# Recurrent core of a two-block network on one core: blocks of one shape put side by side on TensorE, value parts put behind both transposes

## What is computed

```python
def step(S, inp):
    r_t, w_t, k_t, v_t, kk_t, b_t = inp
    sa = jnp.einsum('bhvk,bhk->bhv', S, -kk_t)
    S = S * w_t[:, :, None, :] + sa[..., None] * b_t[:, :, None, :] + v_t[..., None] * k_t[:, :, None, :]
    return S, jnp.einsum('bhvk,bhk->bhv', S, r_t)
...
_, y = lax.scan(step, S0, tuple(to_time(t) for t in (rh, decay, kh, vh, kk, kk * ah)))
```

## Time and profile before

| | us |
|---|---|
| median of 3 runs | 1159.96 |
| lowest, highest | 1159.76, 1161.36 |
| profiled execution, its own time | 1160.52 |
| its span in the profile | 1158.3 |
| groups 0 to 3 of the core in the span | about 91 to 202 |
| PE busy | 1130.8 (98%) |

### The profile page before, as it was taken

One profiled execution on the slowest core, in us unless ns is written; L12 is line 12 of the kernel. 1 busy time (PEld: TensorE's weight loads), 2 busy tenths in 40 slices (PEclk: granted clock), 3 DMA queues, 4 the chain that ended last, 5 costly groups with the idle time before them and its releaser, 6 DMA issues.

```text
span 1158.3 us, 22050 instructions
## 1 busy us (share of the span) xinstructions
PE 1130.8 (98%) x9164; PEld 997.3 (86%) x9164; DVE 818.1 (71%) x1159; ACT 624.8 (54%) x923; POOL 132.3 (11%) x97
## 2 busy tenths in 40 slices
PE   7999999999999999999999999999999999999997
PEld 7797878778888889987888889999998998888886
DVE  7889886377666577898766666888587555666665
ACT  8984664464334455666543344575656655545443
POOL 0032364402300000220031000012000000000000
PEclk9999999999999999999999999999999999999999
DMA  8621211245544654334455447535434333554541
GB/s 306 227 98 51 64 56 57 70 168 183 217 171 165 246 218 146 146 112 180 166 198 218 182 159 267 191 110 218 167 126 151 141 146 145 200 194 171 217 177 41
DMA packets 29796, 187.17 MB, mean 162 GB/s; under 512 B 3472, under 2 KB 5648, under 8 KB 8592
## 3 DMA queue, kind: packets, MB, share of 16 engines
q1 hardware_dynamic: 27072, 177.21, 41.1%
q10 hardware_dynamic: 2640, 8.75, 2.4%
HBM read 184.90 MB, written 1.05 MB: 161 GB/s over the span
## 4 chain that ended last, share of the span: by engine, by line
PE 82%; DVE 10%; ACT 5%; issue 2%; DMA 1%; POOL 0%; DVEq 0%; SPq 0%; ACTq 0%; POOLq 0%
PE ps L2219 16%; PE ps L2201 16%; PE ps L2202 15%; PE ps L2203 15%; PE ps L2220 9%; DVE w_lo L1441 2%; PE ps L2718 1%; PE ps L2571 1%; DVE conv_out L2050 1%; ACT mixed L668 1%; PE ps L2560 1%; PE ps L2499 1%; PE ps L2965 1%; PE ps L2973 1%; PE ps L2451 1%
## 5 line engine op out<-in xcount | busy, mean ns | idle before, releaser
L1441 DVE TENSOR_TENSOR w_lo<-w_raw,w_hi 128x2048 fp32r<-128x2048 f32 x147 | 340.9, 2338 | 84.7 <-ACT w_hi L639 84.6
L639 ACT CAST w_hi<-w_raw 128x2048 fp32r<-128x2048 f32 x144 | 274.2, 1906 | 98.8 <-PE ps L2203 65.0
L2219 PE MATMUL ps<-x_both,w_hi 128*128 128x512 f32 x864 | 302.0, 392 | 1.4 <-DVE x_both L1739 0.6
L2220 PE MATMUL ps<-x_both,w_lo 128*128 128x256 f32 x864 | 243.9, 282 | 0.0
L2219 PEld LDWEIGHTS ps<-x_both,w_hi 128*128 128x128 f32 x864 | 162.2, 188 | 36.5 <-issue 1.5
L2220 PEld LDWEIGHTS ps<-x_both,w_lo 128*128 128x128 f32 x864 | 163.7, 189 | 1.1
L2201 PE MATMUL ps<-x_both,w_hi 128*128 128x256 f32 x432 | 122.0, 282 | 1.6 <-DVE w_lo L1441 0.9
L2202 PE MATMUL ps<-x_both,w_hi 128*128 128x256 f32 x432 | 120.8, 280 | 0.0
L2203 PE MATMUL ps<-x_both,w_lo 128*128 128x256 f32 x432 | 120.8, 280 | 0.0
L2201 PE MATMUL ps<-w_hi,hid_hi 128*128 128x512 f32 x304 | 118.8, 391 | 0.8 <-DVE hid_lo L1867 0.7
L2202 PE MATMUL ps<-w_lo,hid_hi 128*128 128x512 f32 x304 | 118.7, 390 | 0.0
(11 more groups left out here) (443 smaller groups left out, 2109.9 us busy)
## 6 DMA issues: line engine op xcount, KB each, us to landing
w_raw<-in_weights SPq DMA_DIRECT2D x163, 1024.0 KB, 5.0
xt<-in_xT SPq DMA_DIRECT2D x2, 512.0 KB, 5.8
w_raw<-in_weights SPq DMA_DIRECT2D x2, 512.0 KB, 6.6
x_tm<-in_x SPq DMA_DIRECT2D x1, 1024.0 KB, 5.0
gain<-in_mix_g ACTq DMA_DIRECT2D x2, 512.0 KB, 3.6
gain<-in_mix_b ACTq DMA_DIRECT2D x2, 512.0 KB, 5.3
gain<-in_ffn_g ACTq DMA_DIRECT2D x2, 512.0 KB, 5.6
gain<-in_ffn_b ACTq DMA_DIRECT2D x2, 512.0 KB, 9.3
```

Source lines behind the costliest of these rows:

```text
L639: nc.scalar.copy(slab_hi(i), w_raw[:, i % RAW, :]).then_inc(hi_done, 1)
L1441: V.tensor_tensor(slab_lo(i), w_raw[:, i % RAW, :], slab_hi(i).bitcast(F32), ALU.subtract).then_inc(lo_done, 1)
L2219: nc.tensor.matmul(ps[:, bank, :].rearrange("p (s c) -> p s c", s=2), wh, x_both[:, :, k, :], start=start, stop=False)
L2220: return nc.tensor.matmul(ps[:, bank, 0:T], wl, x_hi[:, k, :], start=False, stop=stop)
```

## The change

The loop over the slots on TensorE is written anew, and one entry of `CHAIN_SLOTS` moves. No instruction is added or removed.
- In group 0's even slots the first value part stands behind the transposes of both tiles, no longer between them.
- In slot 2 `C_ST` stands behind the side step instead of ahead of it.
- In slot 4 `C_SB1` stands behind the lower products and ahead of the transposes; before, it stood behind the transposes.
- `C_Y0` moves from the end of slot 4 into slot 5, where it stands behind both tiles' inverse products, directly ahead of `C_Y1`.

ScalarE, VectorE, SyncE and GpSimd keep their order: between `C_SB1` and `C_Y0` ScalarE has nothing but tile 1's turned inverse, and between slots 4 and 5 nothing.

```diff
-        CHAIN_SLOTS = [(C_U0, C_SA0), (C_V0, C_SB0), (C_ST, C_U1), (C_SA1, C_V1), (C_SB1, C_Y0), (C_Y1,)]
+        CHAIN_SLOTS = [(C_U0, C_SA0), (C_V0, C_SB0), (C_ST, C_U1), (C_SA1, C_V1), (C_SB1,), (C_Y0, C_Y1)]
...
+            def lower_products(g, slot, t):
...
+                for h, f, here, there in BLOCKS_64:
+                    mm(level(t, there, crossed(h, f), 0), nt_m[here, t, h], dd[here, t, 0, h], start=True, stop=True)
+
+            def turned_inverse(g, t):
...
+                last.then_inc(inv_ready[t], 1)
+
+            def inverse_products(g, slot, t):
+
+                dd = dd_m[g % 2]
+                pe.wait_ge(inv_taken[t], SLOTS * g + slot)
+                pe.wait_ge(turned_taken[t], (NL - 1) * g + slot // 2 + 1)
...
             for g in range(4):
                 for slot in range(SLOTS):
...
-                        if g == 0 and t == 0:
+                    if slot % 2 == 0:
+                        for t in range(TT):
+                            lower_products(g, slot, t)
+                        if slot == 4:
+                            for step in links[0:1]:
+                                chain_step(*step)
+                            links = []
+                        for t in range(TT):
+                            turned_inverse(g, t)
+                        if g == 0:
                             value_parts(slot, 0)
+                    else:
+                        for t in range(TT):
+                            inverse_products(g, slot, t)
+                            if g == 0 and t == 0:
+                                value_parts(slot, 0)
                     if (g, slot) == (1, 0):
                         pe.wait_ge(proj_taken, 12)
-                    for step in links[0:1]:
-                        chain_step(*step)
+                    if slot not in (2, 5):
+                        for step in links[0:1]:
+                            chain_step(*step)
+                        links = links[1:]
                     for m, k in side_steps(g, slot):
                         side_step(m, k)
-                    for step in links[1:2]:
+                    for step in links:
                         chain_step(*step)
```

More of the change, by code:

```diff
@@ L2536, in value_parts, with level @@
                     v_part(part)
-            SLOT_ORDER = (((0, False), (1, False), (0, True), (1, True)), ((0, False), (1, False)))
+            crossed = lambda h, f: 2 * f + h // 2
+            BLOCKS_64 = [(2 * j + (f ^ x), f, halves_of(f), halves_of(f ^ x)) for j in range(2) for x in range(2) for f in range(2)]
+            def level(t, rows, b, at):
+                return ps[rows, 2 + 2 * t + b // 2, 2 * HB * at + HB * (b % 2):2 * HB * at + HB * (b % 2) + HB]
+            def lower_products(g, slot, t):
+                dd = dd_m[g % 2]
+                if slot == 0:
+                    pe.wait_ge(near_taken[t], g + 1)
+                    wait_side(pe, side_at(g, S_NT))
+                    if g:
+                        pe.wait_ge(inv_taken[t], SLOTS * g)
+                else:
+                    pe.wait_ge(inv_taken[t], SLOTS * g + slot)
+                for h, f, here, there in BLOCKS_64:
+                    mm(level(t, there, crossed(h, f), 0), nt_m[here, t, h], dd[here, t, 0, h], start=True, stop=True)
@@ new lines, in turned_inverse @@
+            def turned_inverse(g, t):
+                dd = dd_m[g % 2]
+                for j in range(2):
+                    for f in range(2):
+                        here = halves_of(f)
+                        last = nc.tensor.transpose(level(t, slice(0, P), 2 * f + j, 1),
+                                                   dd[here, t, 0, 2 * j:2 * j + 2, :].rearrange("p h c -> p (h c)"), ident[here, here])
+                last.then_inc(inv_ready[t], 1)
+            def inverse_products(g, slot, t):
+                dd = dd_m[g % 2]
+                pe.wait_ge(inv_taken[t], SLOTS * g + slot)
+                pe.wait_ge(turned_taken[t], (NL - 1) * g + slot // 2 + 1)
+                for h, f, here, there in BLOCKS_64:
+                    last = mm(level(t, here, 2 * (h % 2) + h // 2, 0), dd[there, t, 1, crossed(h, f)], w_m[there, t, crossed(h, f)],
+                              start=True, stop=True)
+                last.then_inc(inv_ready[t], 1)
@@ L2539, in _ @@
             for g in range(4):
                 for slot in range(SLOTS):
-                    n, dd = slot // 2 + 1, dd_m[g % 2]
                     links = chain_steps(g, slot)
[L2543 to L2563, removed]
-                                for f in range(2):
-                                    here = halves_of(f)
-                                    last = nc.tensor.transpose(level(slice(0, P), 2 * f + j, 1),
-                                                               dd[here, t, 0, 2 * j:2 * j + 2, :].rearrange("p h c -> p (h c)"),
-                                                               ident[here, here])
-                        else:
-                            for h, f, here, there in blocks:
-                                last = mm(level(here, 2 * (h % 2) + h // 2, 0), dd[there, t, 1, crossed(h, f)], w_m[there, t, crossed(h, f)],
-                                          start=True, stop=True)
-                        last.then_inc(inv_ready[t], 1)
-                        if g == 0 and t == 0:
-                            value_parts(slot, 0)
```

1 line of the change is left out of this document (added).

## The result

The forecast was 1163.5 us. The changed kernel takes 1168.03 us, the median of 4 runs (1166.75 to 1169.54), beside 1160.66 (1159.76 to 1161.47) for the kernel before in the same comparison: ratio 1.0058, 95% interval 1.0046 to 1.0071. It is slower, as forecast, but by 0.6% or 7.4 us, twice the 3.5 us forecast, and it lies outside the range. The profiled execution took 1166.75 us.

The account below looks back on a forecast made before the run. TensorE, busy 98% of the span, was taken as the bound. Losses of 1.35 us (slot 2) and 2.7 (slots 4 and 5) less 0.5 (group 0) gave 3.55 more on 1159.96: 1163.5 us, range 1160.2 to 1165.8.

Parts of the forecast that it names:

- group 0: Value parts behind both transposes: fewer turns in slots 0 and 8 save 0.66 us; 0.5 taken, allowing for VectorE.
- What a turn costs: TensorE's change of array shape: entering 0.10 us, leaving 0.09; 0.15 a turn between small shapes.
- Slot 2: C_ST behind the side product in groups 1 to 3: ScalarE's state copies lose cover, 1.35 us lost in sum.
- Slots 4 and 5: Later transposes delay ScalarE's copies and C_Y0 no longer fills the wait: 2.7 us lost over groups 1 to 3.
- nothing holds time back: Behind the core TensorE is the busy engine to the end, so no delay is absorbed there.
- So the shift arrives whole: The core's whole delay, 3.55 us, was to reach the kernel's end.
- TensorE's busy time falls: Sign for the profile after: TensorE's busy time falls while its idle time grows by some 6 us.
- Only the turns count: Rival: nineteen turns go and ScalarE's copies have enough slack; 2.9 us less, 1157.1 us, faster; 10%.
- Slot 2 gains: Rival: later state readers wait no longer, slot 2 brings 0.9 us, slots 4 and 5 lose; 1161.3 us; 20%.
- The delays chain: Rival: later transposes push VectorE's masks, pair takes and GpSimd's input; 6.1 us more in all, 1166.1 us; 8%.

Follow-up runs that it names:

- e4: Kernel before with only group 0's first value part of even slots behind both transposes; median 1159.80 us, ratio 1.0001.
- e1: Kernel before with only C_ST moved behind the side product in slot 2 of groups 1 to 3; median 1162.98 us, ratio 1.0021.
- h: Kernel before with both edits of slots 4 and 5, plus unread matmuls in slot 5 (groups 1, 2) and slot 9 (group 3); 1162.88 us, ratio 1.0014.
- f1: Changed kernel plus unread matmuls in waits of slot 2 (group 2), slot 5 (groups 1, 2) and slot 9 (group 3); 1165.27 us, ratio 1.004.
- e2: Kernel before with only C_SB1 moved ahead of the transposes, C_Y0 left in slot 4; median 1163.09 us, ratio 1.0022.
- e3: Kernel before with only C_Y0 moved to slot 5 behind the inverse products; median 1164.64 us, ratio 1.0027.
- f2: Changed kernel with ScalarE's exponentials moved behind slot 4's copies and VectorE's use of them to slot 5; median 1167.44 us, ratio 1.0059.
- f3: Kernel before with group 0's value parts behind both transposes, C_Y0 in slot 5, and exponentials and their VectorE use moved one slot later; 1160.8 us, ratio 1.0006.
- f4: Kernel before with C_Y0 moved to slot 5, plus three unread matmuls ahead of slot 5's inverse products in groups 1 and 2; 1161.67 us, ratio 1.001.
- g1: Kernel before with group 0's value parts behind both transposes, plus two unread matmuls ahead of slot 9's inverse products in group 3; 1158.91 us, ratio 0.998.
- i: Kernel before with C_ST behind slot 2's side product, plus unread matmuls in slot 2 (group 2) and slot 9 (group 3); 1161.58 us, ratio 1.0001.
- g2: g1 with C_Y0 also moved to slot 5 in group 3 alone; median 1158.92 us, ratio 0.9976.

## Why the prediction was right in direction and short in size

| term, us | sum | changed kernel | apart |
|---|---|---|---|
| group 0 | -0.5 (worked out 0.66) | -0.65 | -0.68 (e4) |
| slot 2: g1, g2, g3 | 0.15, 0.65, 0.55 | 0.23, 0.72, 0.69 | 0.21, 0.72, 0.69 (e1) |
| slots 4, 5: g1, g2, g3 | 0.93, 0.9, 0.85 | 0.75, 0.93, 0.93 | 0.74, 0.94, 0.92 (h) |
| slots 6 to 9 of g3 | 0 | 0.29 | 0 (f1) |
| idle without a releaser, slot 9 of g3 | none | 0.41 | 0 (f1) |
| the clock | none | 1.07 + 1.51 | removed by f1 |
| sum | 3.55 | 6.9 | |

(Group 2's 0.93 is f1's; the changed kernel lost 2.00 there, clock included. The 6.9 is +6.30 less the -0.58 ahead of the core. Of the 0.29, 0.21 is idle time without a releaser in slot 6.)

- **What a turn costs** was right: 2.01 us for slot 0 where 2.03 was worked out. That group 0 as a whole came out at 0.65 is luck in part. VectorE holds back 0.27 at its end, where I had left 0.16, and slot 6 gained 0.23 by a shorter wait, where I had 0.
- **Slot 2** was right in mechanism: the copies begin 0.77 behind C_ST's start (187.07 to 187.84), and the second reader follows them 1.34 later (189.18), for 0.77 and 1.33 in the sum. It was 0.3 short in all. In group 3, C_ST starts 1.38 behind the transposes where the sum had 1.32, and the inverse products follow the second reader by 0.37 where it had 0.3. I had looked for one gap of 0.9 before the second reader; it is two, 0.26 and 0.22, since the first half waits as well. The gap before group 2's side product is there: its row in the changed kernel is

```profile
156.66 1.13 PE L2366 MATMUL ps<-ar,sw 64*128 64x256 f32 x8 [1.20 <-DVE rb L1595]
```

- **Slots 4 and 5** were right: 2.61 where 2.7 was worked out. The gaps are 0.99 and 0.33 in group 1, and 0.19 and 0.33 in group 3 behind the 0.53 ahead of C_SB1.
- **The step that failed** is that the sum prices each wait by its own length alone. The granted clock stands in it at nothing, without a reason, both in group 2 and behind the core ("nothing holds time back", "So the shift arrives whole"). The runs showed 2.6 us of half clock in its place: 1.07 in group 2 and 1.51 of the 1.93 by which +4.37 grew to +6.30 behind slot 9; the other 0.41 is idle time that the sum lacks too. When the clock fell, that cost 1.1 times the wait's length again (1.07 for 0.99 in group 2) to 1.7 times (1.51 for 0.89), and 5 times in e1 (4.5 for 0.89). "TensorE's busy time falls" failed for the same reason.
- **The rivals.** Only the turns count: out by e1 and h. Slot 2 gains: out by e1. The delays chain: its figure, 1166.1, is nearer to the changed kernel's than mine, but by accident. Without the clock and the 0.41, the changed kernel's loss within the core is 3.9 us for the 3.55 of the sum. A chained delay was seen in e2 alone; in the changed kernel all three L1539 take 0.17 us.
- **The median** is 1.3 above the profiled execution. Two of the four runs of the changed kernel stand at a mean granted clock of 0.996 (spans 1164.6 and 1164.8), two at 0.994 (1167.4 and 1166.8). That fits one more low stretch in the latter; they have no profile, so this is argued, not shown.

Open: what decides whether a given wait is followed by a fall. The same 0.89 us ahead of slot 9 was followed by one in the profiles of the changed kernel, e1, e3, f2, f3 and f4, and by none in those of before, e2 and e4. Of the changed kernel's other waits of this length, the 0.99 in slot 5 of group 1 and the 1.20 in slot 2 of group 2 were followed by none.

Open too is how much of g1's gain is the clock's. Over before's best runs (nine at 0.999, 1160.32) it gains 1.4. Group 0's part explains 0.7. In its own profile the core is only 0.19 ahead at the link behind it (+0.14 at the start, -0.05 there), since 0.44 goes in slots 8 and 9 of group 2. But behind the core it gains another 0.7 that is no clock's. There TensorE waits for VectorE (L1548, behind L1441), which works on the weight slab whose load is issued at 225.88. ScalarE's copy of that slab starts 6.27 us behind the issue in before and 4.79 in g1 (issued at 225.83), and TensorE's wait falls from 0.99 to 0.30. ScalarE and TensorE, before and then g1:

```profile
232.15 1.91 ACT L639 CAST w_hi<-w_raw 128x2048 fp32r<-128x2048 f32 x1 [1.99 <-DMA w_raw<-in_weights]
238.43 0.51 PE L2201 MATMUL ps<-w_hi,mix_hi 128*128 128x512 f32 x1 [0.99 <-DVE mix_lo L1548]
```

```profile
230.62 1.91 ACT L639 CAST w_hi<-w_raw 128x2048 fp32r<-128x2048 f32 x1 [0.53 <-DMA w_raw<-in_weights]
237.66 0.50 PE L2201 MATMUL ps<-w_hi,mix_hi 128*128 128x512 f32 x1 [0.30 <-DVE mix_lo L1548]
```

All six kernels with fills have this wait at 0.30 in their profiles, and the eight without at 0.40 to 1.00. So some 0.7 us of what f1, f4, h, i, g1 and g2 gain may be the load's and not the clock's, and why the load lands sooner is not shown. The kernel before with the fills alone, which would part the two, was not run.

## What to carry to other kernels

Where a tuned stretch alternates between TensorE and small copies, look at what each matmul block covers before you sort blocks by shape: here a turn cost 0.1 to 0.2 us, and the cover it took away 0.7 to 0.9. Two edits that are nearly harmless alone can use up the same cover (e2 and e3 in group 3). Price a new wait of TensorE of about 1 us twice: by its length, and by a fall of the clock behind it; fill it with unread matmuls before you judge the order.

## What the runs showed of the hardware

- TensorE's granted clock fell to 1.2 GHz behind waits of only 0.9 to 1.2 us, in a core where it was busy for nine tenths of the time (27.51 of 30 us between 170 and 200). The low stretches lasted from some 3 to 10 us, and cost 1.07 and 1.51 us of the time in the changed kernel and 4.5 in e1. With two to four unread float32 matmuls in each such wait the clock stayed at 2.4 GHz in the profile of f1. The Trainium skill, TensorE: Matmul & The Clock Gate, A second HAM failure mode: psum-queue depth-cycling, describes short idle times of TensorE between groups of matmuls, in every iteration of a loop, with which the clock swings between its two levels. The trace agrees that short idle times are enough; here the clock fell behind single waits of about 1 us.
- The mean granted clock of a run goes with most of the spread of this kernel's times: the 35 runs of before beside e1 have a median of 1159.99 us at 0.999 (seven), 1161.74 at 0.997 (five) and 1165.84 at 0.992 (two). Seven thousandths of 1158 us are 8.1 us; 5.85 of them show in the time.
- An 8-column VectorE instruction took 1.07 and 0.46 us instead of 0.17 where it started 1.04 and 0.43 us before the end of a GpSimd instruction, and ended within 0.03 us of that end (e2).
- ScalarE's copy of a weight slab, which waits for its load, started 6.27 us behind the load's issue in before and 4.79 in g1; what decides it is open.
